# Expert blocks of 32 rows in four partition quarters in place of 64 rows in two halves

## The reference, cut to what matters

```python
N_EXPERTS, TOP_K, D_FF = 32, 4, 1024          # D_MODEL = 1024, SEQ = 512

def moe(h, router_w, router_b, w_up, b_up, w_down, b_down):
    logits = (xt @ router_w + router_b).astype(jnp.float32)
    top_vals, top_idx = lax.top_k(logits, TOP_K)
    gates = jax.nn.softmax(top_vals, axis=-1)
    ...                                        # the 2048 (token, expert) rows, sorted by expert
    def expert_block(args):
        e, xb = args
        hu = xb @ w_up[e] + b_up[e]            # w_up[e]: 1024 x 2048
        g = jnp.minimum(hu[:, :D_FF], SWIGLU_LIMIT)
        lin = jnp.clip(hu[:, D_FF:], -SWIGLU_LIMIT, SWIGLU_LIMIT)
        glu = g * jax.nn.sigmoid(SWIGLU_ALPHA * g)
        return ((lin + 1.0) * glu) @ w_down[e] + b_down[e]     # w_down[e]: 1024 x 1024
    ...                                        # times the gates, summed per token
```

## Time and profile before

| | |
|---|---|
| median of 3 runs | 3463.58 us (3461.01 to 3466.46) |
| span of the profiled execution | 3463.4 us |
| TensorE busy | 2956.5 us, 85% |
| VectorE, ScalarE, GpSimd busy | 1236.1, 840.0, 297.3 us |
| granted TensorE clock, mean | 0.919 |
| DMA over the span | 590.20 MB, 170 GB/s |

### The profile page before, as it was taken

One profiled execution on the slowest core, in us unless ns is written; L12 is line 12 of the kernel. 1 busy time (PEld: TensorE's weight loads), 2 busy tenths in 40 slices (PEclk: granted clock), 3 DMA queues, 4 the chain that ended last, 5 costly groups with the idle time before them and its releaser, 6 DMA issues. The chain is left out here.

```text
span 3463.4 us, 49188 instructions
## 1 busy us (share of the span) xinstructions
PE 2956.5 (85%) x18194; PEld 2124.8 (61%) x18195; DVE 1236.1 (36%) x2541; ACT 840.0 (24%) x1681; POOL 297.3 (9%) x318
## 2 busy tenths in 40 slices
PE   5988666989998878999993778899999878899998
PEld 4965565545554434555552656678887656678886
DVE  1246544211221111212125355543334256544443
ACT  2233221111111101111112124432223124442222
POOL 1000000121112121121212100000000100000000
PEclk8996586999999999999996888899999978999999
DMA  6242005898989999588984210012222210012221
GB/s 175 87 172 78 1 13 218 326 381 317 362 334 374 366 394 364 199 333 319 369 324 173 73 58 1 25 57 96 95 96 96 73 52 1 25 49 97 97 98 49
DMA packets 284547, 590.20 MB, mean 170 GB/s; under 512 B 27572, under 2 KB 55669, under 8 KB 283909
## 3 DMA queue, kind: packets, MB, share of 16 engines
q1 hardware_dynamic: 271796, 561.43, 44.2%
q0 software_dynamic: 8528, 26.58, 2.1%
q10 hardware_dynamic: 4098, 0.49, 0.1%
HBM read 571.17 MB, written 17.30 MB: 170 GB/s over the span
## 5 line engine op out<-in xcount | busy, mean ns | idle before, releaser
L1873 PE MATMUL moe_up<-ring,hT 128*64 128x256 f32 x3360 | 382.7, 386 | 28.2 <-DMA ring<-in_exp_w_up 26.6
L1894 PE MATMUL moe_down<-expert_w,hT 128*64 128x512 f32 x1568 | 356.2, 596 | 53.4 <-ACT hT L1936 32.0
L1873 PEld LDWEIGHTS moe_up<-ring,hT 128*64 128x64 f32 x3360 | 251.1, 139 | 164.3 <-issue 55.9
L1894 PEld LDWEIGHTS moe_down<-expert_w,hT 128*64 128x64 f32 x1568 | 111.2, 137 | 239.7 <-issue 185.7
L1873 PE MATMUL moe_up<-expert_w,hT 128*64 128x256 f32 x1568 | 186.7, 392 | 24.4 <-DMA expert_w<-in_exp_w_up 24.4
L1929 ACT ACTIVATE hT<-hT 128x256 f32<-128x256 f32 x98 | 40.8, 416 | 665.0 <-DVE hT L1952 665.0
L358 PE MATMUL mlp_bank<-hT_hi,mlp_w 128*128 128x512 f32 x512 | 199.6, 390 | 0.0
L359 PE MATMUL mlp_bank<-hT_lo,mlp_w 128*128 128x512 f32 x512 | 199.4, 389 | 0.0
L360 PE MATMUL mlp_bank<-hT_hi,mlp_w 128*128 128x512 f32 x512 | 199.3, 389 | 0.0
L358 PE MATMUL mlp_bank<-mlp_w,mlp_u_hi 128*128 128x512 f32 x512 | 199.3, 389 | 0.0
L359 PE MATMUL mlp_bank<-mlp_w,mlp_u_hi 128*128 128x512 f32 x512 | 199.3, 389 | 0.0
(11 more groups left out here) (508 smaller groups left out, 5380.1 us busy)
## 6 DMA issues: line engine op xcount, KB each, us to landing
ring<-in_exp_w_up SPq DMA_DIRECT2D x64, 2048.0 KB, 10.9
expert_w<-in_exp_w_down SPq DMA_DIRECT2D x64, 2048.0 KB, 10.5
expert_w<-in_exp_w_up SPq DMA_DIRECT2D x32, 2048.0 KB, 10.9
moe_w<-in_exp_w_up SPq DMA_DIRECT2D x32, 2048.0 KB, 11.1
ring<-in_w_ff SPq DMA_DIRECT2D x32, 2048.0 KB, 8.4
ring<-in_ada_w SPq DMA_DIRECT2D x12, 2048.0 KB, 10.6
ring<-in_w_in SPq DMA_DIRECT2D x6, 2048.0 KB, 13.6
ring<-in_w_in SPq DMA_DIRECT2D x10, 1024.0 KB, 6.1
```

The costliest lines, as they stand in the source:

```text
L1873: mm = nc.tensor.matmul(up[c][halves[h], 0:UNITS], rowsT[:, j % 4, halves[j // 4]], chunk[u][c][:, j, h * UNITS:(h + 1) * UNITS], start=(j ...
L1894: mm = nc.tensor.matmul(down[halves[h], :], hidT[:, 2 * half + j % 2, halves[j // 2]], chunk[u][4 + half][:, j, h * COL:(h + 1) * COL], st ...
```

## The change

Blocks have 32 rows. The 128 partitions are four quarters: partition 32 q + r has columns 256 q to 256 q + 255 of row r. Every up or down step is four matmuls of 32 stationary columns, one for each quarter of the output columns, with 128 (up) or 256 (down) moving columns in place of 256 and 512. The tiles of rows, `rowsT`, hidden rows and `y` are half as wide; there are two transposes for the rows and one for each half of the hidden units. The down halves are cut in pieces (`down_rows`), and `turn_hidden(b, 1)` moves ahead of the rest of the first down half; the rows' turn moves into the second. ScalarE takes the rows after both hidden copies. The biases are loaded by five DMAs in place of four and spread by four broadcasts in place of two, to 128, 96, 64 and 32 partitions. Routing counts blocks with an addition and a shift. The chunks of weights, their buffers and the rules of their loads stay.

```diff
--- before.py
+++ after.py
@@ -52,9 +52,11 @@
 ...
 NE, TOPK, FF = 32, 4, 1024
-BR = 64
+BR = 32
+PARTS = P // BR
 MAXB = S * TOPK // BR + NE
-UNITS = FF // 4
+UNITS = COL // PARTS
+YCOLS = D // PARTS
 ALPHA, LIMIT = 1.702, 7.0
@@ -1685,9 +1688,10 @@
 ...
             chain(nc.vector.tensor_copy(count[:], c_bank[:, 0:NE]))
-            chain(nc.vector.tensor_scalar(blocks[:], count[:], 0.0, None, ALU.is_gt))
-            for n in range(1, S // BR):
-                chain(nc.vector.scalar_tensor_tensor(blocks[:], count[:], float(n * BR), blocks[:], ALU.is_gt, ALU.add))
+            chain(nc.vector.tensor_scalar(blocks[:], count[:], float(BR - 1), None, ALU.add))
+            chain(nc.vector.tensor_copy(blocks_i[:], blocks[:]))
+            chain(nc.vector.tensor_single_scalar(blocks_i[:], blocks_i[:], int(math.log2(BR)), ALU.arith_shift_right))
+            chain(nc.vector.tensor_copy(blocks[:], blocks_i[:]))
             chain(nc.vector.tensor_tensor_scan(ends[:], k.ones[:, 0:NE], blocks[:], 0.0, ALU.mult, ALU.add))
 ...
@@ -1756,13 +1760,14 @@
 ...
-        rows, y = k.hT[:, 0, :], k.hT[:, 1, :]
-        rowsT, hidT = (k.hT[:, n, :].rearrange("p (j r) -> p j r", r=P) for n in (2, 3))
-        gate, lin, sig, hid = (k.hT[:, n, :].rearrange("p (h n) -> p h n", n=UNITS) for n in range(4, 8))
+        rows, y = k.hT[:, 0, 0:YCOLS], k.hT[:, 1, 0:YCOLS]
+        rowsT, hidT = (k.hT[:, n, 0:2 * P].rearrange("p (j r) -> p j r", r=P) for n in (2, 3))
+        gate, lin, sig, hid = (k.hT[:, n, 0:2 * UNITS].rearrange("p (h n) -> p h n", n=UNITS) for n in range(4, 8))
         index, place = sb("index", [P, 1], U32), sb("place", [P, 1], U32)
         used_mod = k.mod[:, 0:3, :].rearrange("p n d -> p (n d)")
-        bias, bias_row = sb("bias", [P, 3 * COL]), [used_mod[0:1, h * 3 * COL:(h + 1) * 3 * COL] for h in range(2)]
+        bias_width = 4 * UNITS + YCOLS
+        bias, bias_row = sb("bias", [P, bias_width]), used_mod[0:1, 0:PARTS * bias_width].rearrange("p (q n) -> p q n", n=bias_width)
         bias_loaded, bias_spread, indexed, waited = (sem(s) for s in ("bias_loaded", "bias_spread", "indexed", "waited"))
 ...
@@ -1774,10 +1779,10 @@
 ...
         block = ctx.enter_context(nc.Block())
-        b_up = a["exp_b_up"][0].rearrange("e (s h n) -> e s h n", h=2, n=UNITS)
-        b_down = a["exp_b_down"][0]
-        h2_halves = h2_dram.rearrange("s (h n) -> (s h) n", h=2)
-        y_halves = y_dram.rearrange("s (h n) -> (s h) n", h=2)
+        b_up = a["exp_b_up"][0].rearrange("e (m q n) -> e q m n", q=PARTS, n=UNITS)
+        b_down = a["exp_b_down"][0].rearrange("e (q n) -> e q n", q=PARTS)
+        h2_parts = h2_dram.rearrange("s (q n) -> (s q) n", q=PARTS)
+        y_parts = y_dram.rearrange("s (q n) -> (s q) n", q=PARTS)
@@ -1788,13 +1793,13 @@
 ...
             def load_bias(e):
-                for h in range(2):
-                    sp.dma_start(bias_row[h][:, 0:2 * COL].rearrange("p (s n) -> p s n", n=UNITS), b_up[bass.ds(e, 1), :, h, :]).then_inc(bias_loaded, 16)
-                    sp.dma_start(bias_row[h][:, 2 * COL:], b_down[bass.ds(e, 1), h * COL:(h + 1) * COL]).then_inc(bias_loaded, 16)
+                for q in range(PARTS):
+                    sp.dma_start(bias_row[:, q, 0:4 * UNITS].rearrange("p (m n) -> p m n", n=UNITS), b_up[bass.ds(e, 1), q, :, :]).then_inc(bias_loaded, 16)
+                sp.dma_start(bias_row[:, :, 4 * UNITS:], b_down[bass.ds(e, 1), :, :]).then_inc(bias_loaded, 16)
 ...
-                sp.wait_ge(bias_spread, e * 2)
+                sp.wait_ge(bias_spread, e * PARTS)
                 load_bias(e)
 ...
@@ -1819,7 +1824,7 @@
 ...
                 pool.sem_inc(waited, 1)
-                pool.indirect_dma_start(rows, None, h2_halves,
+                pool.indirect_dma_start(rows, None, h2_parts,
                                         bass.IndirectOffsetOnAxis(ap=index[:], axis=0)).then_inc(gathered, 16)
 ...
@@ -1827,21 +1832,22 @@
 ...
                 pool.sem_inc(waited, 1)
-                pool.indirect_dma_start(y_halves, bass.IndirectOffsetOnAxis(ap=place[:], axis=0), y, None).then_inc(y_stored, 16)
+                pool.indirect_dma_start(y_parts, bass.IndirectOffsetOnAxis(ap=place[:], axis=0), y, None).then_inc(y_stored, 16)
 ...
             with pool.Fori(0, NE) as e:
-                pool.wait_ge(bias_loaded, e * 64 + 64)
+                pool.wait_ge(bias_loaded, e * (16 * (PARTS + 1)) + 16 * (PARTS + 1))
 ...
-                nc.gpsimd.partition_broadcast(bias[:], bias_row[1]).then_inc(bias_spread, 1)
-                pool.wait_ge(bias_spread, e * 2 + 1)
-                pool.sem_inc(waited, 1)
-                nc.gpsimd.partition_broadcast(bias[0:BR, :], bias_row[0], channels=BR).then_inc(bias_spread, 1)
+                for n, q in enumerate(reversed(range(PARTS))):
+                    if n >= 1:
+                        pool.wait_ge(bias_spread, e * PARTS + n)
+                        pool.sem_inc(waited, 1)
+                    nc.gpsimd.partition_broadcast(bias[0:BR * (q + 1), :], bias_row[:, q, :], channels=BR * (q + 1)).then_inc(bias_spread, 1)
                 with pool.Fori(first_block(pool, e), first_block(pool, e + 1)) as b:
 ...
@@ -1859,7 +1865,7 @@
 ...
             def turn_rows():
-                for j in range(4):
+                for j in range(2):
                     tr = nc.tensor.transpose(turn_r[:, j * P:(j + 1) * P], rows[:, j * P:(j + 1) * P], k.ident[:])
 ...
@@ -1869,31 +1875,31 @@
 ...
-                    for h in range(2):
-                        mm = nc.tensor.matmul(up[c][halves[h], 0:UNITS], rowsT[:, j % 4, halves[j // 4]],
-                                              chunk[u][c][:, j, h * UNITS:(h + 1) * UNITS], start=(j == 0), stop=(j == ND - 1))
+                    for q in range(PARTS):
+                        mm = nc.tensor.matmul(up[c][quarter[q], 0:UNITS], rowsT[:, j % 2, quarter[j // 2]],
+                                              chunk[u][c][:, j, q * UNITS:(q + 1) * UNITS], start=(j == 0), stop=(j == ND - 1))
                 mm.then_inc(chunk_done, 1)
 ...
                 pe.wait_ge(hid_taken, b * 2 + (half + 1))
-                for j in range(2):
-                    tr = nc.tensor.transpose(turn_h[half][:, j * P:(j + 1) * P], hid[:, half, j * P:(j + 1) * P], k.ident[:])
-                tr.then_inc(hid_turned, 1)
-
-            def down_half(e, u, b, half):
-                pe.wait_ge(hid_taken, b * 2 + (half + 3))
-                if half == 0:
+                nc.tensor.transpose(turn_h[half][:, 0:P], hid[:, half, :], k.ident[:]).then_inc(hid_turned, 1)
+
+            def down_rows(e, u, b, half, j0, j1):
+                if half == 0 and j0 == 0:
                     pe.wait_ge(y_ready, b + 1)
-                pe.wait_ge(loaded[4 + half], e * 16 + 16)
-                for j in range(4):
-
-                    for h in range(2):
-                        mm = nc.tensor.matmul(down[halves[h], :], hidT[:, 2 * half + j % 2, halves[j // 2]], chunk[u][4 + half][:, j, h * COL:(h + 1) * COL],
+                if j0 == 0:
+                    pe.wait_ge(hid_taken, b * 2 + (half + 3))
+                    pe.wait_ge(loaded[4 + half], e * 16 + 16)
+                for j in range(j0, j1):
+
+                    for q in range(PARTS):
+                        mm = nc.tensor.matmul(down[quarter[q], 0:YCOLS], hidT[:, half, quarter[j]], chunk[u][4 + half][:, j, q * YCOLS:(q + 1) * YCOLS],
                                               start=(half == 0 and j == 0), stop=(half == 1 and j == 3))
-                mm.then_inc(chunk_done, 1)
+                if j1 == 4:
+                    mm.then_inc(chunk_done, 1)
 ...
@@ -1907,17 +1913,19 @@
 ...
                         up_chunk(e, u, b, 3)
-                        down_half(e, u, b, 0)
+                        down_rows(e, u, b, 0, 0, 2)
+                        turn_hidden(b, 1)
+                        down_rows(e, u, b, 0, 2, 4)
+                        down_rows(e, u, b, 1, 0, 2)
 ...
                         turn_rows()
-                        turn_hidden(b, 1)
-                        down_half(e, u, b, 1)
+                        down_rows(e, u, b, 1, 2, 4)
 ...
             def take_rows():
-                nc.scalar.activation(rowsT, turn_r[:].rearrange("p (j r) -> p j r", r=P), ACT.Copy).then_inc(rows_taken, 1)
+                nc.scalar.activation(rowsT, turn_r[:, 0:2 * P].rearrange("p (j r) -> p j r", r=P), ACT.Copy).then_inc(rows_taken, 1)
 ...
@@ -1928,13 +1936,11 @@
 ...
                     for half in range(2):
-                        if half == 1:
-
-                            act.wait_ge(rows_turned, b + 2)
-                            take_rows()
                         act.wait_ge(hid_turned, b * 2 + (half + 1))
-                        nc.scalar.activation(hidT[:, 2 * half:2 * half + 2, :], turn_h[half][:, 0:2 * P].rearrange("p (j r) -> p j r", r=P),
-                                             ACT.Copy).then_inc(hid_taken, 1)
```

(10 more changed lines are left out.)

11 lines of the change are left out of this document (6 added, 5 removed).

## The result

The changed kernel takes 3578.6 us (median, 3577.6 to 3582.2) against 3465.0 (3461.0 to 3466.8) for the kernel before on the same chip: ratio 1.033, 95% interval 1.0317 to 1.0342. It is 3.3% slower. The forecast was 3528 us, so the sign was right and the size 50 us short.

What follows compares the result with a forecast made beforehand. TensorE's work and the weight loads were taken as two close limits. First blocks, further blocks and expert 0 summed to 1289 us, plus 10 for the clock: stage 1300 against 1236, +64, so 3528 us; range 3478 to 3630.

Steps and rivals of the forecast that it cites:

- A block is 12.0 us: TensorE, a 32-row block: up 7.0, down 3.5, transposes 0.5, stall 0.7, gaps 0.3, together 12.0 us.
- Rival (a): Up matmuls: four tiles do not keep up; chunk 3.5 us, near 4025 us, or mildly 2.1 us, 3625 us; chance 0.18.
- The loads do not shrink: Expert weight loads: first blocks cost 19.9 us behind three or more blocks, 21.4 behind two, 33.4 behind one.
- Expert 0's first block: Start of the expert stage: weights are already there, so this block costs 14.3 us.
- The note on the bias: Bias broadcasts in first blocks: 0 to 1 us an expert, taken as 0; 5 us without the late chunk 5.
- The gaps of 0.3 us: TensorE, within each block: small gaps add 0.3 us to the block's sum.
- The clock, 10 us: TensorE in first blocks: idling lowers its clock, at most 52 us in all, mostly covered; 10 taken.
- waits for in_exp_w_down before chunk 5: Sign on TensorE: every first block ends in a wait for this load, some 18 us in.
- TensorE's busy time: Sign in the expert stage: it falls by 150 us and more while the stage grows.
- SP's wait for moe_up: Sign on SP, which issues the weight loads: its wait for TensorE's up matmuls stays near 300 us.
- (c): Weight loads go without a gap because shorter blocks free chunks sooner: stage 1063 us, total 3290 us; chance 0.05.
- (b): TensorE's loop code no longer fits its store, so 15 jumps back wait for fetches: 3570 us; chance 0.07.

Runs made afterwards that it cites:

- e2: Kernel after with every up matmul 256 columns wide instead of 128, same instructions, the second 128 columns useless work: 3844 us.
- e3: Kernel after with the same sums in half the up instructions, each matmul taking 128 gate and 128 linear columns: 3587 us, ratio 1.0346.
- e5: Kernel after without the weight loads of experts 1 to 31, all computing with expert 0's weights: 3457 us, measured once.
- e6: Kernel before without the weight loads of experts 1 to 31, all computing with expert 0's weights: 3364 us, measured once.
- e4: Kernel after with one bias broadcast for an expert instead of four, so three quarters get a wrong bias: 3605 us, measured once.
- e10: Kernel of e5 with TensorE's expert loop written once for all 32 experts instead of as two copies, the same work from half the code: 3460 us.
- e12: Kernel after with chunks 0 and 1 in matmuls of 128 gate and 128 linear columns, second bias buffer, second copy of chunk 2: 3525 us, ratio 1.0183.
- e7: Kernel before with only the new order of down matmuls, transposes and ScalarE's copies, blocks still 64 rows: 3462.2 us, 0.9986.

## Why the prediction was right in sign and short in size

The sum of the stage, term by term, from the table (forecast, then measured): 16 first blocks behind three or more 318, 327; 9 behind two 193, 187; 6 behind one 200, 203; 47 further blocks 564, 617; expert 0's first block 14.3, 22.6; clock 10, held in the others. 1300 against 1356. The total, 3578.6 us, also lies within the forecast's own bounds (3475 to 3590), but not by its terms: their upper end was a block of 12.6 us and the full clock loss, and the block is longer than that. That the sum still stayed under 3590 is luck.

- *A block is 12.0 us*: this step failed. It is 13.13, and 47 of them make the 53 us that are missing. Chunk 3, the down matmuls and the stall behind chunk 3 were sized right; chunks 0 to 2 were taken at 1.75 us because two tiles keep up in the kernel before, which says nothing of instructions at four times the rate. What the runs show in its place are two pauses of 0.4 us a block, cause open. Rival (a) had the size, 2.1 us a chunk, but not the mechanism: the tiles don't slow each other (chunk 3, e2, e3). Its full form, a chunk of 3.5 us, is refuted: a chunk at the full rate takes 1.77 us, 27 ns for a matmul record and its load. The 62 ns a matmul of the Trainium skill's page "TensorE: Matmul & The Clock Gate" (Wait — 56ns, not 53.3ns?) don't bind here either, counted by records or by matmuls of two records (54.5 ns); that page of the Trainium skill gives them for decoding in software, and no trace here says which decoding ran.
- *The loads do not shrink*: its three terms hold within 4% (318, 193 and 200 for 327, 187 and 203), and chunk 5 lands 17.7 us after the last block's end (median behind three blocks and more; 17.8 forecast), with TensorE waiting for it. But the reason is only half of the truth: with no loads at all, 104 of the 119 us stay (e5, e6). I priced the bias ("Without the late chunk 5 it would be 5 us an expert") and set it aside as covered; it is covered, and it also means that the loads cover it.
- *Expert 0's first block*: 22.6 us for 14.3. It has no loads to wait for and pays the bias openly: TensorE waits 6.84 us before the first hidden transpose, and chunk 3 behind it takes 3.2 us for 1.77. The note on the bias had 5 us; I didn't apply it to this one block.
- *The gaps of 0.3 us*: the change of expert, up to 1.7 us, was not in the sum. Loads cover it in most first blocks; in e5 31 gaps of 1.2 to 1.7 us against the overlap of 0.2 within an expert are 44 us.
- *The clock, 10 us*: the total can't be told from the trace; its mechanism is stronger than I had it, and e4 shows that what counts is where the idle time lies.
- *Signs*: chunks of 1.75 (one in four), waits for in_exp_w_down before chunk 5 (30 of 31 first blocks, 39.5 us in all, held; the row's 51.8 us take in waits for chunk 4); TensorE's busy time fell by 36 us, not 150 (half-clock matmuls and most of each pause, bridged by records of 273 ns, count as busy); SP's wait for moe_up was to stay near 300 us and grew:

```profile
SPq L1808 <- PE moe_up L1879: 526.6, 50, 47.5
```

so loads now wait longer for TensorE than before, which is the opposite of (c). (b) fell: from 700 us to the stage's end the code queue moved one packet (at 746 us), and e10, with half the code, is no faster. (I had counted 15 jumps back; the loop over blocks jumps too, 47 times more, for that one packet.) That agrees with the Trainium skill's page "Runtime: NRT & Kernel Launch" (Instruction fetch mechanics) as to 128 KiB for TensorE, and not with its window of two pages, by which every jump back over a body of 42 KB would fetch (an estimate: 648 instructions, at the 256 that the same section of the Trainium skill counts in 16 KiB).

## What to carry to other kernels

A block of half the rows isn't half a block: what an expert costs once (its bias, its last weights, the sequencer's work between loops) was hidden under 23 us and isn't under 13. So before halving a tile list every cover by its length, also those that two waits share, since in first blocks behind three and more removing one of them alone lost 1.4 us (e4) or bought 0.8 (e5), and taking at both bought 3.3 (e12). And a saving on the path is worth what comes next: e3 and e7 each gave back in a chain or a load what they won.

## What the runs showed of the hardware

- Four column tiles of 32 stationary columns run side by side, fp32: four records of 128 columns every 109 ns.
- At that rate TensorE pauses for 0.3 to 0.4 us at certain records (91 and about 150 of a further block, 46 to 50 or none of a first one in the same code); with 256 columns a matmul it doesn't. When the first of them ends, the sequencer is some 16 records ahead (an estimate from 21 records 0.45 us later and 11 ns an instruction). The cause is open.
- The sequencer runs 16 to 24 matmul records with their loads ahead, so 2.3 us of register work are free behind 16 records of 512 columns on two tiles (3.5 us), and 1.7 us of it cost 1.0 behind 16 of 256 columns on four (0.9 us).
- A partition broadcast takes 1.05 us for 768 columns and 1.80 for 1536, for 32 partitions as for 128.
- Less work can be slower: behind an idle time of 2.9 us late in a block the last 48 down records ran at the lower clock, 32 of them with nothing to cover them (e4); behind one of 3.5 us early in the block (the kernel after) those that ran slowly were covered by the loads.
